# The second expert layer's outputs joined to the residual by one-hot products on TensorE

## What is computed, cut to what matters

```
hb = silu(xb @ w_gate[e]) * (xb @ w_up[e])
y  = (hb @ w_down[e]) * gate[:, None]
h  = h + zeros.at[slot_tok].add(y)
out = rmsnorm(h, g_final)
```

## Time and profile before

| | us |
|---|---|
| median of 3 runs | 1872.3 |
| lowest and highest | 1868.67, 1878.84 |
| the profiled execution, its own time | 1877.97 |
| its span | 1876.1 |
| PE busy, share of the span | 1575.6 (84%) |
| DVE busy | 745.4 (40%) |
| ACT busy | 333.6 (18%) |
| bytes moved by DMA | 412.02 MB |

### The profile page before, as it was taken

One profiled execution on the slowest core, in us unless ns is written; L12 is line 12 of the kernel. 1 busy time (PEld: TensorE's weight loads), 2 busy tenths in 40 slices (PEclk: granted clock), 3 DMA queues, 4 the chain that ended last, 5 costly groups with the idle time before them and its releaser, 6 DMA issues.

```text
span 1876.1 us, 18635 instructions
## 1 busy us (share of the span) xinstructions
PE 1575.6 (84%) x7428; PEld 1031.5 (55%) x7428; DVE 745.4 (40%) x1201; ACT 333.6 (18%) x558; POOL 266.1 (14%) x311
## 2 busy tenths in 40 slices
PE   5996999897899697788699978998788887887882
PEld 4685888785788442333588866767633332332330
DVE  6899645526355511111732338875320000000003
ACT  3310100115200210000311155751110000000001
POOL 0102003300000130110200014762020000000001
PEclk9998999999999798899799988988899998999986
DMA  4232122220135799999322200004789999999993
GB/s 168 76 110 70 64 94 90 90 71 20 46 138 213 283 370 413 427 428 397 148 90 83 96 1 1 1 1 173 313 313 430 429 429 430 429 430 429 431 408 152
DMA packets 54818, 412.02 MB, mean 220 GB/s; under 512 B 13888, under 2 KB 15168, under 8 KB 25936
## 3 DMA queue, kind: packets, MB, share of 16 engines
q1 hardware_dynamic: 45008, 394.05, 52.3%
q0 software_dynamic: 9728, 16.81, 2.4%
HBM read 402.40 MB, written 25.20 MB: 228 GB/s over the span
## 4 chain that ended last, share of the span: by engine, by line
PE 53%; DMA 26%; DVE 10%; ACT 4%; POOL 3%; issue 2%; SPq 2%; POOLq 0%; DVEq 0%; ACTq 0%
PE bank L1428 33%; PE bank L647 8%; DMA arena<-in_expert_gate 5%; DMA arena<-in_expert_in 5%; DMA arena<-in_expert_up 5%; DMA arena<-in_expert_down 5%; PE bank L657 3%; DMA ring<-in_expert_up 2%; DMA arena<-in_expert_out 1%; DVE arena L2149 1%; PE bank L1543 1%; DVE top L2148 1%; DVE ring_low L2044 1%; PE bank L1420 1%; ACT misc L1800 1%
## 5 line engine op out<-in xcount | busy, mean ns | idle before, releaser
L647 PE MATMUL bank<-arena 128*64 128x512 f32 x960 | 286.1, 656 | 76.8 <-DMA arena<-in_expert_up 22.4
L647 PEld LDWEIGHTS bank<-arena 128*64 128x64 f32 x960 | 96.2, 151 | 249.1 <-issue 246.5
L647 PE MATMUL bank<-ring,arena 128*64 128x512 f32 x576 | 182.4, 624 | 25.1 <-DMA ring<-in_expert_up 9.5
L895 DVE TENSOR_TENSOR arena<-misc,bank 128x256 f32<-128x256 f32 (+1 forms) x32 | 17.7, 554 | 443.4 <-PE bank L647 305.4
L2043 DVE CAST ring_high<-ring 128x2048 fp32r<-128x2048 f32 x60 | 75.9, 1265 | 262.1 <-DMA ring<-in_stream_a 158.5
L2044 DVE TENSOR_TENSOR ring_low<-ring,ring_high 128x2048 fp32r<-128x2048 f32 x60 | 140.8, 2347 | 2.1
L657 PE MATMUL bank<-arena 128*64 128x512 f32 x448 | 116.1, 603 | 20.7 <-issue 11.8
L1428 PE MATMUL bank<-ring_low,xn_high 128*128 128x512 f32 x288 | 113.3, 393 | 0.0
L1428 PE MATMUL bank<-ring_high,xn_low 128*128 128x512 f32 x288 | 112.6, 391 | 0.0
L1428 PE MATMUL bank<-ring_high,xn_high 128*128 128x512 f32 x288 | 112.6, 391 | 0.0
L647 PEld LDWEIGHTS bank<-ring,arena 128*64 128x64 f32 x576 | 60.4, 144 | 90.0 <-issue 90.0
(11 more groups left out here) (373 smaller groups left out, 2845.6 us busy)
## 6 DMA issues: line engine op xcount, KB each, us to landing
ring<-in_stream_a SPq DMA_DIRECT2D x42, 1024.0 KB, 5.0
arena<-in_expert_gate SPq DMA_DIRECT2D x20, 2048.0 KB, 28.4
arena<-in_expert_up SPq DMA_DIRECT2D x20, 2048.0 KB, 28.1
arena<-in_expert_in SPq DMA_DIRECT2D x19, 2048.0 KB, 26.9
arena<-in_expert_down SPq DMA_DIRECT2D x18, 2048.0 KB, 28.9
ring<-in_expert_up SPq DMA_DIRECT2D x12, 2048.0 KB, 32.0
ring<-in_expert_down SPq DMA_DIRECT2D x12, 2048.0 KB, 29.7
ring<-in_expert_gate SPq DMA_DIRECT2D x12, 2048.0 KB, 31.0
```

Of the source, the lines that this page charges most:

```text
L647: last = nc.tensor.matmul(h[side * SLOTS:(side + 1) * SLOTS, :], tokens[:, k, side * SLOTS:(side + 1) * SLOTS], w[:, k * 512:(k + 1) * 512 ...
```

## The change

Only the second layer (`m.b == 1`) is changed. `y_rows`, its stores and its loads are no longer used there. Instead:

- Once, in pair 0: DVE makes a row of token numbers 0 to 511 (eight small operations), a float copy of the token table, and the product of the router's hits with the gates (`m.tagged`, issued in the router's rest). PE makes the gate of every slot by products with `in_slot` (`gate_products_pe`, 16 calls of 128x16, after the up part of pair 0), and DVE copies them to `gate_slot`.
- For each pair p: DVE makes `spread`, a one-hot matrix of 128 slots by 512 tokens (`spread_dve`). ACT takes banks 6 and 7 out with the gate as scale into `y_high` (fp32r), DVE takes them again and subtracts, into `y_low` (`low_dve`).
- PE then multiplies: a unit is one token tile t and one half of the columns, two fp32r matmuls of 128x512 (`spread` with `y_high`, then with `y_low`) into bank 5. Eight units make a pair. DVE adds each unit to the residual (`add_dve`, 128x512), and the next unit waits for this, as there is one bank.
- The units of pair p-1 run inside pair p: after every second k step of the gate part one unit (n = 0 to 3), and ahead of the up part's wait for its tiles four in a row (n = 4 to 7). Those of pair 15 run after its `down`, over six banks.
- The sum is complete with the last addition; the final norm follows as before. Some tables in SBUF change places to make room (`levels`, `le`).

The core of the diff; the overflow path, whose body is also rewritten, is left out:

```diff
+        COMBINE_BANK = 5
+        LAST_BANKS = (5, 0, 1, 2, 3, 4)
+        def units_before(p):
+            return 1 + 2 * NT * p
+        def spread_pe(pe, m, p, n, bank_at):
+            t, half = divmod(n, 2)
+            pe.wait_ge(m.y_low_ready, 3 * p + 2 + half)
+            w = spread[:, p % 2, t * P:(t + 1) * P]
+            nc.tensor.matmul(bank[bank_at][:, :], w, half_of(y_high[:, p % 2, :], half), start=True, stop=False)
+            nc.tensor.matmul(bank[bank_at][:, :], w, half_of(y_low[p % 2], half), start=False, stop=True)\
+                .then_inc(m.combined, 1)
+        def gate_products_pe(pe, m):
+            pe.wait_ge(exp_in, 3 * m.b + 4)
+            for side in range(2):
+                for n in range(2 * NT):
+                    last = nc.tensor.matmul(bank[COMBINE_BANK][side * SLOTS:(side + 1) * SLOTS, 0:PAIRS], m.in_slot[:, n, :],
+                                            m.tagged[:, n, side:NE:2], start=(n == 0), stop=(n == 2 * NT - 1))
+            last.then_inc(m.combined, 1)
...
-            last.then_inc(done, 1)
+                if k == KC - 1:
+                    last.then_inc(done, 1)
+                if between and k % 2 == 1:
+                    between(k // 2)
...
+                def spread_unit(n, p=p):
+                    pe.wait_ge(m.moe_added, units_before(p - 1) + n)
+                    spread_pe(pe, m, p - 1, n, COMBINE_BANK)
...
+                    if m.b == 1 and p >= 1 and part == 0:
+                        between = spread_unit
+                    if m.b == 1 and p >= 1 and part == 1:
+                        for n in range(NT, 2 * NT):
+                            spread_unit(n)
...
+                if m.b == 1 and p == 0:
+                    gate_products_pe(pe, m)
...
+            if m.b == 1:
+                for n in range(2 * NT):
+                    pe.wait_ge(m.moe_added, units_before(PAIRS - 1) + max(0, n - len(LAST_BANKS) + 1))
+                    spread_pe(pe, m, PAIRS - 1, n, LAST_BANKS[n % len(LAST_BANKS)])
...
+                    for half in range(2):
+                        act.wait_ge(m.y_done, 2 * p + half + 1)
+                        A.activation(half_of(y_high[:, q, :], half), bank[6 + half][:, :], ACT.Copy,
+                                     scale=gate_slot[:, p:p + 1]).then_inc(m.y_high_ready, 1)
...
+        def low_dve(dve, m, p):
+            for half in range(2):
+                dve.wait_ge(m.y_high_ready, 2 * p + half + 1)
+                V.scalar_tensor_tensor(half_of(y_low[p % 2], half), bank[6 + half][:, :], gate_slot[:, p:p + 1],
+                                       half_of(y_high[:, p % 2, :], half).bitcast(F32), ALU.mult, ALU.subtract)\
+                    .then_inc(m.y_low_ready, 1)
+        def add_dve(dve, m, p, n, bank_at):
+            t, half = divmod(n, 2)
+            dve.wait_ge(m.combined, units_before(p) + n + 1)
+            place = half_of(x[:, t, :], half)
+            nc.vector.tensor_tensor(place, place, bank[bank_at][:, :], ALU.add).then_inc(m.moe_added, 1)
...
+                if m.b == 1 and p >= 1:
+                    dve.wait_ge(m.moe_added, units_before(p - 1))
+                    for n in range(2 * NT):
+                        add_dve(dve, m, p - 1, n, COMBINE_BANK)
...
             moe_sp(sp, m, rows_of_end, lambda: None)
-            combine_sp(sp, m)
```

More of the change, by code:

```diff
@@ L68, in constant_table @@
     put("strict", np.where(row < col, 0.0, NEG))
+    levels = []
+    for lv in range(LEVELS):
+        h = P >> (lv + 1)
+        same = (row // (2 * h)) == (col // (2 * h))
+        levels.append((same & ((row // h) % 2 == 0) & ((col // h) % 2 == 1)) * 1.0)
+    levels.append((row == col) * 1.0)
+    put("levels", np.concatenate(levels, axis=1))
     put("pad_rows", np.where(row >= P - META, 0.0, NEG)[:, :1])
@@ L638, in build, with half_of, gate_up @@
         moes = [Moe(0, 2), Moe(1, 4)]
-        def gate_up(h, m, tokens, tiles, done, arrived=None):
+        gate_slot = sb("gate_slot", [P, PAIRS])
+        token_f = sb("token_f", [P, PAIRS])
+        over_home = sb("over_home", [SLOTS, 2])
+        spread = part("spread", cst_place, CONST_COLS["levels"][0], [2, SEQ])
+        spread_over = part("spread_over", cst_place, CONST_COLS["tri_ge"][0], [1, SEQ])
+        y_high = part("y1_high", arena_place, 0, [2, D])
+        y_low = [part("y1_low0", misc_place, 0, [1, D])[:, 0, :], part("y1_low1", misc_place, 2048, [1, D])[:, 0, :]]
+        iota_token = router_w[:, :, :].rearrange("p k s -> p (k s)")
+        COMBINE_BANK = 5
+        LAST_BANKS = (5, 0, 1, 2, 3, 4)
+        def half_of(v, half):
+            return v[:, half * 512:(half + 1) * 512]
+        def units_before(p):
[14 more added lines that the diff above has]
+            last.then_inc(m.combined, 1)
+        def gate_up(h, m, tokens, tiles, done, arrived=None, between=None):
             for k in range(KC):
@@ L772, in over_pe @@
                     down(m, m.over_hidden, [m.over_slots[m.parts]], m.over_y)
-                    pe.wait_ge(m.over_y_act, v + 1)
-                    pe.wait_ge(m.over_y_dve, v + 1)
-                    alone(pe)
+                    if m.b == 0:
+                        pe.wait_ge(m.over_y_act, v + 1)
+                        pe.wait_ge(m.over_y_dve, v + 1)
+                        alone(pe)
+                    else:
+                        pe.wait_ge(m.over_y_dve, v * 6 + 6)
+                        alone(pe)
+                        for n in range(4 * NT):
+                            k, t, half = n // (2 * NT), n % (2 * NT) // 2, n % 2
+                            if n >= 1:
+                                pe.wait_ge(m.over_added, v * 16 + n)
+                                alone(pe)
+                            w = (spread[0:SLOTS, 1, :], spread_over[0:SLOTS, 0, :])[k][:, t * P:(t + 1) * P]
+                            nc.tensor.matmul(bank[COMBINE_BANK][:, :], w, half_of(y_high[0:SLOTS, 1, :], half),
+                                             start=True, stop=False)
+                            nc.tensor.matmul(bank[COMBINE_BANK][:, :], w, half_of(y_low[1][0:SLOTS, :], half),
+                                             start=False, stop=True).then_inc(m.over_combined, 1)
+                        pe.wait_ge(m.over_added, v * 16 + 16)
+                        alone(pe)
         def moe_pe(pe, m):
@@ L882, in moe_dve @@
+        def add_dve(dve, m, p, n, bank_at):
+            t, half = divmod(n, 2)
+            dve.wait_ge(m.combined, units_before(p) + n + 1)
+            place = half_of(x[:, t, :], half)
+            nc.vector.tensor_tensor(place, place, bank[bank_at][:, :], ALU.add).then_inc(m.moe_added, 1)
+        def moe_dve(dve, m, before, combined, route_rest, then):
             V = nc.vector
@@ L900, in moe_dve @@
                     .then_inc(m.actT_ready, 1)
[L901 to L904, removed]
+                if m.b == 0:
+                    dve.wait_ge(m.y_done, 2 * p + 2)
+                    if p >= 2:
+                        dve.wait_ge(m.y_stored[q], 16 * (p // 2))
+                    V.tensor_copy(m.y[:, q, 512:1024], bank[7][:, :]).then_inc(m.y_free_dve, 1)
+                else:
+                    if p == 0:
+                        for i in range(KC):
+                            then(V.tensor_scalar(router_w[:, i, :], c("iota_slot"), float(i * SLOTS), None, ALU.add))
+                        then(V.tensor_copy(token_f[:, :], m.token_table[:, :]))
+                    spread_dve(dve, m, p)
+                    if p == 0:
+                        dve.wait_ge(m.combined, 1)
+                        V.tensor_copy(gate_slot[:, :], bank[COMBINE_BANK][:, 0:PAIRS]).then_inc(m.moe_added, 1)
+                        dve.wait_ge(m.moe_added, 1)
+                    low_dve(dve, m, p)
                 if p == OVER_AFTER:
@@ L908, in moe_dve @@
             before()
+            if m.b == 1:
+                dve.wait_ge(m.moe_added, units_before(PAIRS - 1))
+                for n in range(2 * NT):
+                    add_dve(dve, m, PAIRS - 1, n, LAST_BANKS[n % len(LAST_BANKS)])
+                    combined(n)
+                return
             for n in range(2 * NT):
```

160 lines of the change are left out of this document (113 added, 47 removed).

## The result

The changed kernel takes 1937.0 us (median of 4 runs, 1934.8 to 1941.8) against 1870.5 for the kernel before beside it (4 runs, 1868.7 to 1878.8): ratio 1.034 [1.031, 1.036], 66.5 us slower. Its profiled execution took 1934.79 us with a span of 1932.8; the one before had 1877.97 and 1876.1, so profile to profile the difference is 57 us. (Over 23 later runs the kernel before has a median of 1873.8, so its profiled execution was a long one.) In the changed kernel L690 is the gate and up line, L703 and L716 the down part, L670 and L671 the two products of a unit, L1035 DVE's addition of a unit, L1060 DVE's copy of the transposed hidden rows, L2663 DVE's scaling in the final norm.

The account below looks back on a forecast made before the run. The weight stream bound the kernel, with PE next and becoming the bound. Pairs and loop +46, clock +12, pair 0 +2 and end -12 gave +48 us on the 1872.3 median: 1920 us, range 1882 to 1950.

Parts of the forecast that it names:

- parts 1 and 2: Units between gate k steps and in the row before up: 9.4 us more a pair (bounds 7.6 and 11.4).
- Need without units: PE's own time for a pair at full clock, without the added units: 23.4 us.
- Form changes: Switching PE's array between 128*64 and 128*128 around units: 0.2 us a change, bounds nothing and 0.4.
- part 3: Empty overflow loop behind pair 6: PE's standing still, hidden before, now costs 7.75 us.
- part 4: Clock falls behind the row of four units in about half of the pairs: 12 us, bounds none and 38.
- part 5: Pair 0: its added gate products cost 2 us; the extra DVE work there lies beside the down part.
- part 6: ACT's copies, DVE's subtractions and additions stay hidden; removed stores, 0.67 us each, count nothing unless the weights bind.
- part 7: From the last down part to the last norm: 14 us in place of 26.5, so 12 us less.
- A: The clock holds through the rows of units: 36 us slower, 1908 us; chance 0.22.
- B: Clock falls in nearly every pair, or form changes cost twice as much: 1945 us; chance 0.2.
- C: Units run inside waits for weights, the stream stays the bound, rounds about one us: 1852 us; chance 0.08.
- D: Added time at its lower bound of 7.6 us a pair and the clock holds: 1875 to 1881 us; chance 0.08.

Follow-up runs that it names:

- experiment 4: Changed kernel with units 4 to 7 of pairs 0 to 14 and their additions left out: 1852.7 us, ratio 0.989.
- experiment 3: Changed kernel with three unread products into free bank 1 ahead of each of units 4 to 7: 1907.1 us, ratio 1.020.
- experiments 5 and 6: Second layer's empty overflow loop left out, of the changed kernel (1923.5 us, ratio 1.027) and of the kernel before (1875.9 us, ratio 1.001).
- experiments 7 and 8: experiment 1 with one unread store per pair put back (1860.0 us, ratio 0.994), and experiment 1 without the second layer's overflow loop (1849.0 us, ratio 0.987).
- experiment 1: Changed kernel with units 4 to 7 in banks 0, 1, 4 and 5, not all in bank 5: 1851.2 us, ratio 0.989.
- experiment 2: Changed kernel with units 4 to 7 also between k steps, of the up part, still through one bank: 1872.1 us, ratio 0.998.

## Why the prediction was right, and the step that was mis-sized

Forecast 1920 with 1882 to 1950, measured 1937. The mechanism is the one that happened; one term of the sum was off. By the profiled executions the forecast is 1926 against 1934.8, which looks closer only because the work ahead of the layer and the last store were 7.3 us shorter in the one after.

- **PE becomes the bound (parts 1 and 2): right, and of the size forecast.** Need without units 23.4: measured 23.4 (experiment 4). A unit between k steps 0.86: measured 0.81 (the k steps on both sides of it start 2.53 apart, of which 1.72 are theirs). A round 1.46: measured 1.52, the first product 0.34 ahead of the second where I had 0.31. From the gate to the up part 6.8: measured 7.2, of which 0.5 is the last unit at the low clock. At full clock the pair takes 32.73 (experiment 3) where 32.8 stood in the forecast. (The pairs that I called 7 and 8 there are pairs 9 and 10: the gate part of pair 7 is the one behind the loop, at 1575.34. Nothing in the sum hangs on it.)
- **Form changes:** with 0.46 for a unit in a row and 0.81 between k steps, a change costs 0.17 against my 0.2. The letter of Key Properties in the page TensorEngine Tiling (Array Packing) of the Trainium skill, taken as a full drain at each entry into a unit, would have added 0.8 us a pair; no run shows that.
- **The loop (part 3): right.** 8.0 in place of 7.75, paid in the changed kernel, free before (experiments 5 and 6). The low clock behind it, about 2 us, was not in the sum.
- **The clock (part 4): the mis-sized term.** I expected the fall "in about half of the pairs: 7.5 x 1.6 = 12 us". It came in all 15. The up parts lose 19.4 us, and the last unit of each row another 0.4 to 0.5 (from its start to the up part 1.15 us, 1756.73 to 1757.88, against 0.67 in experiment 3, 1642.16 to 1642.83), and in pairs 2 and 12 the unit ahead of it 0.5 as well, together 27 to 28; experiment 3 gives 28 by the stretch and 30 by the medians. With this the stretch closes: 15 x 32.73 + 8.0 for the loop + 2 for the clock behind it + 27.5 = 528.5, as measured. I had a single stretch of such rounds for it, in another stage. They were of nearly this length (0.66 us of work after 0.83 idle, against 0.74 and 0.78), and the clock fell behind them; I halved the price without a reason from a row. The rows of the 15 pairs are alike, so that all or none was the likelier outcome than one half.
- **Pair 0 (part 5): right, in part by luck.** +2.4 against +2. The gate products ran at full clock, 1.78 us in place of 3.17, and add 1.7. The remaining 0.7 us is in the gate part of pair 0, for which I had no term: its first 33 entries take 9.62 us against 8.85 in the kernel before, at a mean granted clock of 0.76 against 0.83.
- **Hidden work (part 6): right.** The stores counted nothing in the changed kernel, which doesn't wait for the stream. They are worth 0.6 to 0.8 us each once the stream binds (experiments 7 and 8), around the 0.67 read from their share.
- **The end (part 7): right.** 13.5 us against 14.

The rivals: A (the clock holds) fell, but its 1908 is near what experiment 3 measures (1907) when the clock is made to hold; that the two agree so well is luck, as experiment 3 has the long pair 0 in it. B (the clock falls in nearly every pair, 1945) is what happened, and 8 us high: it counted some 37 us for the clock where 27 to 28 came. The section A second HAM failure mode: psum-queue depth-cycling of the Trainium skill's page TensorE: Matmul & The Clock Gate spoke for it, and this trace agrees, with a fall in every row of rounds. C (the units hide in the waits for weights) needed rounds of one us and got 1.52; it is, though, nearly the picture of experiment 1: 1852 was its figure, 1851 is measured. D fell with the lower bound of 7.6: 9.3 came.

What stays open: the up part takes 7.9 to 8.5 us in most pairs and 9.5 in two of them (pairs 1 and 11). The trace shows how: over the first 7 us of those two parts the mean granted clock is 0.65 and 0.63, in the others 0.79 to 0.87. Why the low clock lasts longer there, and why it falls a unit early in the pair behind each, it doesn't show. Of the distances between the units of the row only none and two k steps (experiment 2) were tried.

## What to carry to other kernels

When work is put into another engine's waits, price the round trip and not the work: four units of 0.46 us cost 1.5 each because one bank made each wait for DVE's addition of the one before, and three banks that were free made the same work fit. Where a row of rounds like this one (some 6 us, half of each round idle) stands in the plan, count the lower clock behind every such row and not behind some, as it came in 15 of 15 here, and read what a stall costs from the engine that binds after the change: the loop's 8 us were free before and paid after. A wait that the binding resource covered is no slack that can be spent twice.

## What the runs showed of the hardware

- The granted clock fell to the 1.2 GHz level in every one of 15 rows of four rounds of 1.52 us with 0.78 idle in each, and cost 0.4 to 1.0 us in the row and 0.9 to 2.6 in the part behind it. Three products ahead of each unit, read by nobody, kept it at 1.00 and made the kernel 30 us faster (experiment 3).
- fp32r products of 128x512 start 0.23 us apart in a stream (experiment 1), but the second starts 0.34 behind the first where the first follows a wait or fp32 work of another form.
- The empty loop of 15 turns costs PE 8.0 us of issue, and about 2 more at the low clock behind it. With the stream binding, neither shows in the time (1875.9 against 1873.8 us).
- One indirect store of a pair's rows costs a stream at 430 GB/s 0.6 to 0.8 us (experiment 7 against 1 and 8).
